# Stick-breaking heads and the first gate tiles by the seven-product block scheme, with cached keys and values in eight shared slots

## The reference

```
xn = RMSNorm(x)
rq rk rv rg sq sk sv sg gr gs = split(xn @ w_in)          # w_in 2048 x 14336
o_ret = retention(rope(rq), rope(rk), rv)                 # 8 heads, 128 -> 256
o_sb  = stick_breaking(sq, sk, sv, bias)                  # 8 heads of 128
h = x + (sig(gr) * ((GN(o_ret)*silu(rg)) @ w_ret) + sig(gs) * ((o_sb*silu(sg)) @ w_sb)) @ w_out
stick_breaking: z = q.k/sqrt(d) + bias_h;  A[t,s] = sig(z[t,s]) * prod_{s<j<t} (1 - sig(z[t,j])),  s < t
```

## Time and profile before

| what | before |
|---|---|
| median of three runs | 2182.64 us (2181.4 to 2182.66) |
| the profiled execution, its own time | 2180.88 us |
| its span | 2179.1 us |
| PE busy | 2126.3 us, 98%, 16152 instructions |
| weight loads (beside PE) | 2052.5 us, 94% |
| DVE busy | 1270.2 us, 58% |
| ACT busy | 891.4 us, 41% |
| POOL busy | 113.6 us, 5% |
| granted clock of PE, mean | 0.989 of full |
| DMA | 271.74 MB, mean 125 GB/s |

### The profile page before, as it was taken

One profiled execution on the slowest core, in us unless ns is written; L12 is line 12 of the kernel. 1 busy time (PEld: TensorE's weight loads), 2 busy tenths in 40 slices (PEclk: granted clock), 3 DMA queues, 4 the chain that ended last, 5 costly groups with the idle time before them and its releaser, 6 DMA issues.

```text
span 2179.1 us, 43110 instructions
## 1 busy us (share of the span) xinstructions
PE 2126.3 (98%) x16152; PEld 2052.5 (94%) x16152; DVE 1270.2 (58%) x1675; ACT 891.4 (41%) x1330; POOL 113.6 (5%) x161
## 2 busy tenths in 40 slices
PE   5999999999999999999999999999999999999996
PEld 4999999999999999999999999999999999999995
DVE  4334442444357567788788788788787854442223
ACT  5334332433243445444444444444455632222223
POOL 4011100111010000000000000000000000000000
PEclk7999999999999999999999999999999999999998
DMA  4444434444433434423333433433446444543333
GB/s 143 136 124 136 132 113 130 129 134 118 122 94 122 149 110 132 130 78 113 119 110 112 119 110 112 119 110 112 120 130 203 145 138 150 164 131 99 106 101 131
DMA packets 454446, 271.74 MB, mean 125 GB/s; under 512 B 22498, under 2 KB 436450, under 8 KB 453090
## 3 DMA queue, kind: packets, MB, share of 16 engines
q1 hardware_dynamic: 452194, 265.99, 41.3%
q10 hardware_dynamic: 2176, 4.72, 0.6%
HBM read 232.89 MB, written 37.75 MB: 124 GB/s over the span
## 4 chain that ended last, share of the span: by engine, by line
PE 94%; DVE 1%; DVEq 1%; POOL 1%; ACT 1%; ACTq 0%; DMA 0%; issue 0%; SPq 0%; POOLq 0%
PE ACC L630 45%; PE ACC L861 25%; PE ACC L867 12%; PE Z L650 4%; PE Z L700 1%; PE Z L776 1%; POOL XL L2011 1%; PE Z L714 1%; PE Z L905 1%; PE Z L682 1%; PE Z L750 1%; PE Z L889 1%; PE Z L980 1%; PE Z L914 1%; PE Z L891 0%; DMA XN<-in_x_prompt 0%
## 5 line engine op out<-in xcount | busy, mean ns | idle before, releaser
L1502 DVE TENSOR_TENSOR LO<-RAW,HI 128x512 fp32r<-128x512 f32 x304 | 212.9, 701 | 377.2 <-ACT HI L1074 356.3
L1236 ACT ACTIVATE HI<-RAW 128x1024 fp32r<-128x1024 f32 x266 | 274.7, 1053 | 354.9 <-PE ACC L867 203.5
L1690 DVE TENSOR_TENSOR LO<-RAW,HI 128x1024 fp32r<-128x1024 f32 x266 | 324.6, 1229 | 148.4 <-ACT HI L1236 133.8
L630 PE MATMUL ACC<-XH,HI 128*128 128x288 f32 x1664 | 366.6, 302 | 10.1 <-POOL XL L2011 6.5
L630 PE MATMUL ACC<-XH,LO 128*128 128x288 f32 x1664 | 356.8, 296 | 0.0
L630 PE MATMUL ACC<-XL,HI 128*128 128x288 f32 x1664 | 356.6, 296 | 0.0
L1074 ACT ACTIVATE HI<-RAW 128x512 fp32r<-128x512 f32 x304 | 190.5, 629 | 367.9 <-PE ACC L630 330.6
L861 PE MATMUL ACC<-XH,HI 128*128 128x288 f32 x1216 | 329.9, 297 | 1.0 <-ACTq L1258 1.0
L861 PE MATMUL ACC<-XL,HI 128*128 128x288 f32 x1216 | 326.8, 295 | 0.0
L630 PEld LDWEIGHTS ACC<-XH,HI 128*128 128x128 f32 x1664 | 266.6, 190 | 26.6 <-issue 15.0
L630 PEld LDWEIGHTS ACC<-XL,HI 128*128 128x128 f32 x1664 | 268.7, 189 | 0.0
(11 more groups left out here) (252 smaller groups left out, 2847.5 us busy)
## 6 DMA issues: line engine op xcount, KB each, us to landing
RAW<-in_w_in SPq DMA_DIRECT2D x224, 512.0 KB, 3.9
KC<-in_cache_sb_k SPq DMA_DIRECT2D x256, 64.0 KB, 1.9
VC<-in_cache_sb_v SPq DMA_DIRECT2D x256, 64.0 KB, 2.5
RAW<-in_w_ret_proj SPq DMA_DIRECT2D x32, 512.0 KB, 4.2
RAW<-in_w_out SPq DMA_DIRECT2D x32, 512.0 KB, 3.9
RAW<-in_w_sb_proj SPq DMA_DIRECT2D x16, 512.0 KB, 3.9
ST<-in_state_ret SPq DMA_DIRECT2D x64, 128.0 KB, 2.7
out<-ST SPq DMA_DIRECT2D x64, 128.0 KB, 3.1
```

The lines of the kernel that those rows point to most:

```text
L630: mm = pe.matmul(ACC[a][:, half, 0:HALF], w[:, s // 2, s % 2 * QK + k, :], x[:, k0 + k, half * HALF:(half + 1) * HALF], start=first and k ...
L1236: act.activation(HI[:, SLOT[n]], RAW[:, SRC[n]], ACT.Copy).then_inc(S["hi_made"], 1)
L1502: dve.tensor_tensor(LO[:, s // 2, part, :], RAW[:, r, (n % 2) * QK:(n % 2 + 1) * QK, :], HI[:, s // 2, part, :].bitcast(F32), ALU.subtract ...
L1690: dve.tensor_tensor(LO[:, SLOT[n]], RAW[:, SRC[n]], HI[:, SLOT[n]].bitcast(F32), ALU.subtract)\
```

## The change

- Stick-breaking heads 1 to 7 make their four tiles as two pairs (query with key into `QK_`, value with gate into `VG`), and the gate tiles `C_GS` 0 to 5 are made as three pairs, two with the attention of head 7 and one after it, ahead of `w_sb`. Five gate pairs follow `w_sb`. Head 0 stays direct.
- The attention's steps are now placed after the 14 products of the two pairs; ACT and DVE have step tables of their own (`sb_attention(n)`).
- The block sums and differences of x are made during head 0.
- Cached keys and values share eight slots, `KV`; transposed keys go back to the slot that they came from. Values are issued after the logits that read the keys, the next head's keys after the values' product.
- The gated branch of a head goes to DRAM (`d_b`), and is read back once ahead of `w_sb`. The gate's sigmoid is made by ACT (absolute value, exponential, logarithm, exponential) in place of DVE's reciprocal.
- New keys and new values are written out separately.

The core of the diff (in the parts that only move, lines are left out):

```diff
-        PAIRS = 6 + 3 * H + 8
+        PAIRS = 2 * (H - 1) + 8 + 3 * H + 8
...
-        KC, at = sb("KC", [P, NB, 4 * P], at=t_at)
-        VC, at = sb("VC", [P, NB, 4 * P], at=at)
-        KTR, at = sb("KTR", [P, 4, 4 * P], at=at)
+        KV, at = sb("KV", [P, NB, 4 * P], at=at)
...
+            def second_pair_loads(h, c1, c2, step):          # SP
+
+                upper_blocks(w_in[0], c1, c2, step)
+                new_rows_out(VN, sbv_p, sbv_s, h - 1, "vn", "v_out")
+                t.past("z_act3", 2)
+                t.settle()
+                for b in range(4):
+                    values(h - 1, b)
+                lower_blocks(w_in[0], c1, c2, step)
+                t.past("z_act3", 4)
+                t.settle()
+                for b in range(4, 8):
+                    values(h - 1, b)
...
+            def sb_loads(h, c1, c2, step):
+
+                second_pair_loads(h, C_SV, C_SG, h)
+                upper_blocks(w_in[0], c1, c2, step)
+                new_rows_out(KN, sbk_p, sbk_s, h, "kn", "k_out")
+                lower_blocks(w_in[0], c1, c2, step)
+                t.past("z_dve3", 3)
+                t.settle()
+                for b in range(8):
+                    keys(h, b)
+                branch_out(h)
...
             def sb_attention(q):                             # PE
                 if q == 0:
+                    pe.wait_ge(S["h0_ev"], 2)
...
                 if q == 6:
                     t.room("z_read2")
                     suffix(2, 0, [3])
                     suffix(3, 256, []).then_inc(S["z_dve2"], 1)
                 if q == 6:
                     group_logits(1)
...
+            def sb_head(first, new):                         # PE
+                for u in range(2):
+                    def after(n):
+                        if first and u == 0 and n in (0, 2):
+                            pe.wait_ge(S["lows_made"], 3 + n // 2)
+                        sb_attention(7 * u + n)
+                        if new and 7 * u + n == 8:
+                            t.past("comb", 0)
+                            new_keys()
+                    pair(after)
...
+            def sb_attention(n):                             # DVE
+                if n == 3:
+                    odd_keys(1)
+                    for o, m in SEG:
+                        log_keep(o, o + m)
+                    new_values()
+                if n == 4:
+                    odd_keys(3)
+                if n == 6:
+                    odd_keys(5)
+                    less_later(0)
+                if n == 7:
+                    odd_keys(7)
+                    less_later(1)
+                    t.take("ln_made")
+                    dve.scalar_tensor_tensor(GG[:, :], VG[:, 1, :], 0.0, GG[:, :], ALU.min, ALU.subtract)\
+                        .then_inc(S["gate_raw"], 1)
+                if n == 8:
+                    less_later(2)
+                if n == 9:
+                    log_keep(ZS0, ZW)
+                    t.take("sig_made")
+                    dve.tensor_tensor(GG[:, :], GG[:, :], VG[:, 1, :], ALU.mult)
+                    dve.drain()
...
+            def sb_head(new, first=False):                   # DVE
+                for u, dst in enumerate((QK_, VG)):
+                    def after(n):
+                        sb_attention(7 * u + n)
+                        if new and 7 * u + n == 10:
+                            new_keys()
+                        if not new and u == 1:
+                            gate_parts(n, QK_, GS_T)
+                    pair(dst, None if first and u == 0 else (VG, QK_)[u], after)
...
+                if n == 3:                                   # ACT, sb_attention
+                    softplus(0, ZS0, 3)
+                    even_keys(0)
+                if n == 4:
+                    even_keys(2)
+                    t.take("k_out", 32)
+                    for o, m in SEG:
+                        t.take("l_ready")
+                        act.activation(LH[:, o:o + m], LL[:, o:o + m], ACT.Copy).then_inc(S["lh_done"], 1)
...
+            pair(QK_, VG, gate_of_second)                    # DVE, third gate pair
+            splits[0] += 2
+            split()
+            split()
+            finish(QK_)
+            for k in range(0, 8, 2):
+                if k == 4:
+                    split()
+                t.take("rh_done")
+                dve.tensor_tensor(RLB[:, k:k + 2, :], RLR[:, k:k + 2, :], RHB[:, k:k + 2, :].bitcast(F32), ALU.subtract)\
+                    .then_inc(S["lows_made"], 1)
```

More of the change, by code:

```diff
@@ L336, in cached_values @@
[L336 to L349, removed]
-                    keys(h, b)
@@ L352, in sb_body @@
[L352 to L367, removed]
-                t.enter(i, 1, PER_SB)
[L369 to L377, removed]
+                sp.dma_start(prompt[0, 0, :, h, :].rearrange("(n p) d -> p n d", p=P), src[:, 0:4, :])\
+                    .then_inc(S[out], 16)
@@ L396, in _ @@
                 t.leave(3)
[L399 to L430, removed]
+            first_blocks(w_in[0], C_GS + 6 * P, C_GS + 7 * P)
             for c in (13, 14, 15):
@@ L686, in group_back @@
-            def group_back():
-                t.take("zq_ready")
-                t.room("z_read3")
-                for c in range(PAGES):
-                    mm = transpose(Z[3][:, c * P:(c + 1) * P], ZQ[:, c * P:(c + 1) * P])
-                mm.then_inc(S["z_act3"], 1)
-            def suffix(j, col, later):
-                n = BLK[j][1]
-                for jj in (j, *later):
-                    oo, m = BLK[jj]
-                    for part in (LH, LO_):
-                        mm = pe.matmul(Z[2][:, col + n - m:col + n], MATSR[:, 0 if jj == j else 1, :],
-                                       part[:, oo:oo + m], start=jj == j and part is LH,
-                                       stop=jj == (j, *later)[-1] and part is LO_)
-                return mm
@@ new lines, in group_back, with suffix @@
+            def group_back():
+                t.take("zq_ready")
+                t.room("z_read3")
+                for c in range(PAGES):
+                    mm = transpose(Z[3][:, c * P:(c + 1) * P], ZQ[:, c * P:(c + 1) * P])
+                mm.then_inc(S["z_act3"], 1)
+            def suffix(j, col, later):
+                n = BLK[j][1]
+                for jj in (j, *later):
+                    oo, m = BLK[jj]
+                    for part in (LH, LO_):
+                        mm = pe.matmul(Z[2][:, col + n - m:col + n], MATSR[:, 0 if jj == j else 1, :],
+                                       part[:, oo:oo + m], start=jj == j and part is LH,
+                                       stop=jj == (j, *later)[-1] and part is LO_)
+                return mm
@@ new lines, in nothing @@
+            def nothing(n):
+                pass
+            for q in range(16):
+                if q < 4:
+                    pe.wait_ge(S["xh_done"], 17 + q)
+                    pe.wait_ge(S["xl_done"], 17 + q)
+                quarter(XH, XL, q % 4 * 4, q % 4 == 0, q % 4 == 3, "act")
+                if q == 9:
+                    pe.wait_ge(S["h0_ev"], 2)
+                    new_keys()
+            for s in range(2):
+                t.reach(f"acc_read{s}")
+            sb_head(True, True)
@@ new lines, in _ @@
+            with pe.Fori(2, H) as i:
+                t.enter(i, 2, PER_SB)
+                sb_head(False, True)
+                t.leave(H - 2)
+            sb_head(False, False)
+            pair(nothing)
+            t.past("comb", 0)
+            slot[0] += 2
+            for q in range(2):
+                pe.wait_ge(S["lows_made"], 6 + 2 * q)
+                quarter(RHB, RLB, 4 * q, q == 0, q == 1, "act")
+            for p in range(3):
+                unit(RHB, RLB, 0, "act", units=1)
@@ L880, in chunk_outputs @@
+            with pe.Fori(1, 4) as i:
+                t.enter(i, 1, PER_PSB)
+                for p in range(4):
+                    unit(RHB, RLB, 0, "act", units=1)
+                t.leave(3)
             def chunk_outputs(g):
@@ L1188, in sb_body @@
-            def sb_body(a):
-                for q in range(16):
-                    split()
-                    if a is not None:
-                        sb_attention(q, a)
-                    sb_new(q)
-            sb_body(None)
-            with act.Fori(1, H) as i:
-                t.enter(i, 1, PER_SB)
-                sb_body(i - 1)
-                t.leave(H - 1)
-            def gate(s):
-                t.room(f"pg_out{s}", 16)
-                gate_exp(s, SG[:, s, :])
-                act.drain().then_inc(S[f"acc_read{s}"], 1)
@@ new lines, in _ @@
+            split()
+            split()
+            act.wait_ge(S["rl_in"], 64)
+            act.wait_ge(S["v_out"], 32 * H)
+            for k in range(0, 8, 2):
+                if k == 4:
+                    t.past("prod", 0)
+                    split()
```

(18 more changed lines are left out.)

935 lines of the change are left out of this document (475 added, 460 removed).

## The result

The changed kernel takes 2193.83 us (median of 4 runs, 2192.29 to 2196.96); the kernel before took 2182.65 beside it (4 runs, 2181.4 to 2182.74). The ratio is 1.0054, with an interval of 1.0042 to 1.0067: half a per cent slower. The forecast was 2160.5, faster, with a range that ended at 2183. It was wrong in sign and in range.

What follows compares the result with a forecast made beforehand. PE's matmul stream was taken as the bound. 2180.9 - 51.1 (matmuls) + 24.0 (head waits) + 1.9 + 3.3 (hand-overs) - 1.0 + 0.8 (clock) = 2158.8, as a median 2160.5 us; range 2141 to 2183.

Steps and rivals of the forecast that it cites:

- Matmuls removed: Heads 1 to 7 and first four gate tiles: 16 pairs save 384 matmuls, -51.1 us; a head takes 64.9 us.
- the forecast's sum without head waits: Forecast total leaving out PE's waits inside the heads: 2136.6 us with the median.
- Load of the other engines: DVE some 46 and ACT some 36 of 65 us a head; extra load taken as 0.
- The wait behind product 6: First pair of each head: PE awaits DVE's subtraction, queued behind finish(); 2.8 us a head, at least 1.85.
- The logits wait of step 3: PE's logits in each head need DVE's odd key copy of sample 3: 0.2 us a head, bounds 0 and 2.
- The clock: w_sb hand-over +0.8 us; rival: each head's gap halves PE's clock, 10.4 us more, 2171 us, chance 0.20.
- the slow rival: In-order DVE queue: ACT's passes at step 3 start 2 us late, 8.1 us a head, about 2200; chance 0.10.
- Hand-overs: PE waits: head 0 to first pair +1.9 us, last gate pair to w_sb +3.3, last head's reciprocal wait -1.0.

Runs made afterwards that it cites:

- both orders: Changed kernel with DVE's subtraction and its key copy a step earlier, and sample 3's odd key copy ahead of value copies and low part: 2140.39 us, 0.9803 of the kernel before.

## Why the prediction was wrong

**Matmuls removed: right.** A head without waits lasts 64.9 us, as forecast, and with both moves the kernel stands at 2140.4, against 2136.5 in the forecast's sum without head waits. That leaves 3.9 between the medians. Between the profiled executions it is 5.9, and 4.4 of these can be read: 0.9 is the clock behind the w_sb hand-over (that stage takes 103.3 us against 101.6 before, for the same matmuls; 0.8 of these 1.7 was forecast), 0.5 a later start, 1.3 a longer half clock behind the gap ahead of the merge stage (2.8 us lost against 1.5), and 1.7 the half clock behind the 2.0 us gap at the first pair (the mean clock is 0.76 from 99.76 to 106.76). The forecast put nothing on that last one. The rest is open.

**Load of the other engines: right.** DVE is busy 44.5 of 72 us, ACT 33.2; 46 and 36 had been said. Neither bounded anything.

**The wait behind product 6: right in place, cause and number of times, too small in size.** Counted from the end of the first logits (192.28 + 1.10): product 6 ended at +13.9 (211.53 less the 4.21 of the gap), as forecast. a22 was issued at +8.7 and not +8.1, landed after 4.7 and not 4.0, and PE went on at +18.1 and not +16.8. Mean 3.7 in place of 2.8: +6.9 us in all. The landing time had been read in a head with no 16 transfers ahead of the block.

**The logits wait of step 3: mis-sized, +7.0 us.** The lead was counted at 0.3 us with a low part of 1.23. It takes 2.2 to 2.4 beside POOL's subtraction, and PE waits 1.4 in six heads. In the head whose low part stands at 261.00, counted from 245.49, where the prediction's 3.2 us of product begin, PE reached these logits at 17.9 (17.8 forecast) and the copy was done at 19.1 (17.5): of the 1.6, 1.1 is the low part and 0.4 the two value copies with their pauses. The price of the low part was from a stage in which POOL does no such subtraction. The wait lay inside the bounds of 0 to 2.

**The clock: the step that failed.** The prediction says of the head's gap "I leave it out of the sum and make it a rival", at 1.3 us a head and a chance of 0.20, against it "PE works densely on both sides". The windows show 15.1 us, the runs 15.4 and 15.9: 1.9 a head. The gaps were 3.1 to 4.2 us, all eight dropped the clock, and even gaps of 1.9 us did so four times in eight. Dense work on both sides, the reason given against it, did not keep the clock up. The price of 1.3 was also short: it was read from the half clock up to 1743 alone, and behind the gaps of the heads 1.7 us are lost, once 3.2. The Trainium skill ("TensorE: Matmul & The Clock Gate", "HAM oscillation") says that a loop whose waits drop the clock pays for it in every turn; the windows show just that. The forecast quoted that rule, and did not follow it.

**The account.** 2160.5 + 6.9 + 7.0 + 15.5 + 3.9 = 2193.8. The first two terms alone give 2174, still faster; the clock with the forecast's waits gives 2176, still faster; only together do they cross. That is the break-even of the slow rival: 5.8 us a head could be lost, and by the kernel with both orders 53.4 / 8 = 6.7 were. The period by the chain is 71.65 (214.31 to 285.96) against 71.24 before. The slow rival named this place and this sum of three, at 8.1 a head and a chance of 0.10, but another trigger: it had ACT's passes 2 us late. They ended within 0.2 us of the count (DVE's passes on their result began at 12.5 for 12.3, counted as above), and it was DVE's low part that was slow.

**Hand-overs: the waits right**, 2.0, 3.3 and the 1.0 gone; the half clock behind the first was left out and behind the second put at half.

## What to carry to other kernels

When the instruction that frees a PSUM buffer stands in an engine's queue behind a wait for the last product of a group, PE stalls in every turn, however idle that engine is (DVE was busy 63% of the time here): count the instructions between the release and the wait, and move the release, not the load. Price each repeated gap of PE twice, as the wait and as the half clock behind it; here the second was half of the first. A removed wait may not show its size while another gap near it lets the clock fall (2.7 of 8.6 us here, and all of them once the long gap was gone), so mend them together before judging either.

## What the runs showed of the hardware

- A gap of 1.8 to 1.9 us between dense stretches dropped PE to half clock in 4 of 8 equal heads; behind waits of 1.4 us in the heads, and of 1.1 us at the hand-overs, the clock was full. The 2.0 us gap at the first pair dropped it in five of the nine profiles of the changed kernel and its variants.
- The length of a gap does not settle it. The 3.66 us gap ahead of the merge stage cost 2.8 us of half clock in the kernel with both orders, and nothing in the kernel after, where the clock behind it is full:

```profile
1753.00:1755.00 2.00, 1.48 (x11) 1.48 (x12) 1.91 (x4) 2.00 (x3) 0.00 (x0) 1.00 0.63 192
```

- The half clock behind the heads' gaps lasted about 3.4 us or about 6.8, in one and the same kernel too: 6.8 behind a gap of 3.78, 3.4 behind one of 4.21. What decides stays open.
- Adding 25.6 us of matmuls made the kernel 14 us faster.
- A DVE subtraction of 128x1024 that takes 1.23 us took up to 2.35 beside POOL's subtractions. Three of these took from 3.22 to 5.28 us, by the order in which the two engines began.
